# Feed-forward products of a decoder layer: quarters of the tokens (258 columns) in place of thirds (344)

## Chip, cores and metric

The kernel runs on one core of one Trainium2 chip. The metric is the device time of one execution in microseconds (us); the number of a version is the median of several executions. The engines are written PE (TensorE, matrix products), PEld (TensorE's weight loads, which run beside the products), DVE (VectorE), ACT (ScalarE), POOL (GpSimd) and SP (SyncE, which here only issues DMAs).

## The reference, cut to what matters

One inference step of a hybrid decoder layer for a prompt of 1024 tokens and 8 sampled tokens, together T = 1032 tokens, with D_MODEL = 1024 and D_FF = 4096. An input projection, a sparse attention, a state-space branch and a merge come first. The part that the change touches is the feed-forward sub-layer at the end:

```python
def conv_ffn(h, conv_prev, w_up, conv_w, conv_b, w_down):
    up = h @ w_up                                   # (T, 1024) @ (1024, 8192)
    t = up.shape[1]
    ext = jnp.concatenate([conv_prev.astype(up.dtype), up], axis=1)
    acc = conv_b + ext[:, 0:t] * conv_w[0]
    for j in range(1, CONV_W):                      # causal depthwise conv, width 3
        acc = acc + ext[:, j:j + t] * conv_w[j]
    a, b = jnp.split(acc, 2, axis=-1)
    out = (jax.nn.gelu(a) * b) @ w_down             # (T, 4096) @ (4096, 1024)
    return out, ext[:, -(CONV_W - 1):]
```

Its output goes through an RMS norm and is added to the layer's input.

## The kernel before, in words

**Layout.** Activations lie transposed: features on the 128 partitions, the 1032 tokens along the free axis. A product has 128 weights columns as its stationary operand and a run of tokens as its moving operand. Every float32 operand is split in a high part (type fp32r) and the rest (fp32r too), and each product is the sum of three: high by high, high by low, low by high. The split is why every matmul stands three times in the profile, with operands `wh`/`xh`, `wh`/`xl` and `wl`/`xh`.

**project() (line 53; its matmul is recorded as L58).** It makes one unit of output, 128 features by 1032 tokens. The tokens are taken in three chunks of CH = 344 columns; chunk c of the unit in slot s is accumulated in PSUM bank 3s + c. There are two slots, so banks 0 to 5 hold units, and banks 6 and 7 are free for other things. Inside a chunk the loop runs over the kt blocks of 128 input features and the three parts: 3 kt matmuls, each with a weight load of its own in front (PEld). The helper `thirds(ps, slot)` (line 63) views the three banks as one operand for the engine that empties them, and `as_thirds` (line 67) shapes the SBUF side alike.

**phase_ffn (line 2156) and its order.** The 4096 hidden features are taken in NG2 = 16 groups of 256. A group `it` has four "up" units (`ups`, line 2470 on; kt = 8, so 72 matmuls each): a and b halves of two blocks of 128. PE then makes the eight "down" units (`downs`, line 2480 on; kt = 2, so 18 matmuls each) of the group before, which add its 256 hidden features to the 1024 output features. So PE's order is: ups(0), ups(1), downs of group 0, then a hardware loop of 7 turns (`Fori`), two groups a turn, each ups(it) and the downs of it - 1, and at last the downs of group 15. Units alternate between slot 0 and slot 1, and a unit may begin when the one before it in its slot has been emptied.

**Who empties them.** ACT empties an up unit (`evacuate`, L2310) into `up`, and then makes the first of three convolution taps (L2314). DVE makes the other taps (L2380, L2381, L2389), the product of the halves (L2396) and the low part of it (L2401). DVE also empties the down units (`down`, L2410 for the first group, L2412 after): it adds the unit to the running sum `fT`. Where these stand in DVE's queue is written out by hand in `iteration`: down unit 0 goes after the taps of up unit 2; then the middle taps of up unit 3; down unit 1; the last tap of unit 3 and the product; down unit 2; the low part; down units 3 to 7. ACT and POOL make the high and low parts of the streamed weights (L2300, L2254) into two buffers, which SP fills by DMA.

**The end of the phase.** Ten columns of each up unit are kept (POOL, L2261). After the loop PE waits for them, turns eight of the ten by transposes (L2507) into banks 6 and 7, and makes the last eight down units. It then waits until ACT has copied the turned columns (`k_copied`) and turns the other two into bank 7 (L2512). While the last down units come, ACT squares the finished sums, DVE adds the squares up (L2420), PE sums them over partitions into bank 6 (L2516), and at last PE turns `fT` back (L2524), DVE normalises and adds (L2465), and the result is stored. The lines of the end that matter:

```python
            pe.wait_ge(kept_cols, FT)
            for r in range(8):
                mm = pe.transpose(ps[0:FT, 6 + r // 4, (r % 4) * P:(r % 4 + 1) * P], keep[:, r, :], g.ident[:, :])
            mm.then_inc(k_turned, 1)
            downs(NG2, job(NG2, 0), 1, ups_before=False)
            pe.wait_ge(k_copied, 1)
```

Other phases use products of the same type: the input projection with chunks of 344 columns (L1036), the merge (L58 too, with `m_` and `g_y` names), and the output projection (L2112), which has 512 columns a matmul and, for the eight sampled tokens, weights of only 8 columns. L1152 and L1154 are float32 products in the state-space branch, of 128 and of 8 columns.

Of the kernel before, what the change touches and what calls it, by code (L numbers as in the profile page):

```python
# [8 lines left out]
ALU = mybir.AluOpType  # L9
ACT = mybir.ActivationFunctionType  # L10
# [7 lines left out]
KD = D // P  # L18
NP = 1024
NS = 8  # L20
T = NP + NS
# [41 lines left out]
def thirds(ps, slot, m=P):  # L63
    return ps[0:m, 3 * slot:3 * slot + 3, 0:CH]

def as_thirds(ap):
    return ap.rearrange("p (c t) -> p c t", c=3)

def newton_rstd(dve, rstd, std, var, done, base=0):
# [1799 lines left out]
NG2 = FF // P // 2  # L1871
# [284 lines left out]
def phase_ffn(nc, g):  # L2156
# [4 lines left out]
    with ExitStack() as ctx:  # L2161
        sb = lambda n, s, d=F32: ctx.enter_context(nc.sbuf_tensor("f_" + n, s, d))
        ps, sem = g.ps, lambda n: g.sem("f_" + n)
# [119 lines left out]
        def _(act):  # L2283
# [18 lines left out]
            def evacuate(it, q):  # L2302

                u, r = it * 4 + q, q % 2
                tile = bass.ds(it * 2 + (q // 2 + r * (FT // 2)), 1)
                act.wait_ge(up_done, u + 1)
                if not isinstance(it, int) or it or q >= 2:
                    act.wait_ge(conv, u - 1)
                    act.wait_ge(kept_cols, u - 1)
                act.activation(as_thirds(up[:, r, 2:2 + T]), thirds(ps, r), ACT.Copy).then_inc(up_evac, 1)  # L2310
                act.wait_ge(up_evac, u + 1)
                if not isinstance(it, int) or it or q >= 2:
                    act.wait_ge(g_lo, it * 2 + q // 2)
                act.activation(acc[:, r, 0:NP], up[:, r, 0:NP], ACT.Identity, scale=g.cw[:, 0, tile],  # L2314
                               bias=g.cw[:, 3, tile]).then_inc(tap0, 1)
# [58 lines left out]
        @block.vector  # L2374
        def _(dve):
            def tap_mid(it, q):
                u, r = it * 4 + q, q % 2
                tile = bass.ds(it * 2 + (q // 2 + r * (FT // 2)), 1)
                dve.wait_ge(tap0, u + 1)
                dve.tensor_copy(acc[:, r, NP:T], g.conv0[:, tile, :].rearrange("p a b -> p (a b)")).then_inc(tap0s, 1)  # L2380
                dve.scalar_tensor_tensor(out=acc[:, r, 0:NP], in0=up[:, r, 1:1 + NP], scalar=g.cw[:, 1, tile],  # L2381
                                         in1=acc[:, r, 0:NP], op0=ALU.mult, op1=ALU.add).then_inc(tap1, 1)

            def tap_last(it, q):
                u, r = it * 4 + q, q % 2
                tile = bass.ds(it * 2 + (q // 2 + r * (FT // 2)), 1)
                dve.wait_ge(tap0s, u + 1)
                dve.wait_ge(tap1, u + 1)
                dve.scalar_tensor_tensor(out=acc[:, r, :], in0=up[:, r, 2:2 + T], scalar=g.cw[:, 2, tile],  # L2389
                                         in1=acc[:, r, :], op0=ALU.mult, op1=ALU.add).then_inc(conv, 1)  # L2390

            def product(it, r, par):
                m = it * 2 + r
                dve.wait_ge(gelu, m + 1)
                dve.wait_ge(conv, m * 2 + 2)
                dve.tensor_tensor(acc[:, 0, :], acc[:, 0, :], acc[:, 1, :], ALU.mult).then_inc(prod, 1)  # L2396

            def low(it, r, par):
                m = it * 2 + r
                dve.wait_ge(g_hi, m + 1)  # L2400
                dve.tensor_tensor(gl[:, par, r, :], acc[:, 0, :], gh[:, par, r, :].bitcast(F32), ALU.subtract).then_inc(g_lo, 1)  # L2401

            def down(d, m):

                dve.wait_ge(down_done, d + 1)
                if not isinstance(d, int) or d >= 8:
                    dve.wait_ge(down_evac, d - 7)  # L2407
                f = as_thirds(g.fT[:, m, :])
                if isinstance(d, int) and d < 8:
                    dve.tensor_copy(f, thirds(ps, m % 2)).then_inc(down_evac, 1)  # L2410
                else:
                    dve.tensor_tensor(f, thirds(ps, m % 2), f, ALU.add).then_inc(down_evac, 1)  # L2412

            def add_squares(m):

                dve.wait_ge(sq_done, m + 1)
                if m >= 2:
                    dve.wait_ge(sum_done, m - 1)
                other = squares[:, 0, :] if m == 1 else total
                dve.tensor_tensor(total, squares[:, m % 2, :], other, ALU.add).then_inc(sum_done, 1)  # L2420

            def iteration(it, par, has_down):
                for q in range(3):
                    tap_mid(it, q)
                    tap_last(it, q)
                    if q == 1:
                        product(it, 0, par)
                        low(it, 0, par)
                if has_down:
                    down(it * 8 - 8, 0)  # L2430
                tap_mid(it, 3)
                if has_down:
                    down(it * 8 - 7, 1)
                tap_last(it, 3)
                product(it, 1, par)
                if has_down:
                    down(it * 8 - 6, 2)
                low(it, 1, par)
                if has_down:
                    for m in range(3, 8):  # L2440
                        down(it * 8 + (m - 8), m)

            dve.wait_ge(zero, 1)
            iteration(0, 0, False)
            iteration(1, 1, True)
            with dve.Fori(0, (NG2 - 2) // 2) as j:
                for e in range(2):
                    iteration(j * 2 + (2 + e), e, True)
            dve.memset(ones[:, :], 1.0)
            dve.memset(var[:, :], 1.0)  # L2450
            for m in range(8):
                down((NG2 - 1) * 8 + m, m)
                if m >= 2:
                    add_squares(m - 1)
            add_squares(KD - 1)

            dve.wait_ge(ss_done, 1)
            dve.tensor_scalar(var[:, 0:NT], ps[:, 6, 0:NT], 1.0 / D, EPS, ALU.mult, ALU.add).then_inc(ss_copied, 1)
            dve.tensor_scalar(var[0:NS, NT:9], ps[0:NS, 6, NT:9], 1.0 / D, EPS, ALU.mult, ALU.add).then_inc(ss_copied, 1)
            dve.wait_ge(std_done, 1)  # L2460
            newton_rstd(dve, rstd[:, :], std[:, :], var[:, :], r_done, 0)
            for i, (_, n) in enumerate(TILES):
                dve.wait_ge(turned, i + 1)
                dve.wait_ge(x2_in[i % NX], 16 * (i // NX + 1))
                dve.scalar_tensor_tensor(out=x2[0:n, i % NX, :], in0=tile_cols(i), scalar=rstd[0:n, i:i + 1],  # L2465
                                         in1=x2[0:n, i % NX, :], op0=ALU.mult, op1=ALU.add).then_inc(y_done, 1)

        @block.tensor
        def _(pe):
            def ups(it, q, j, s):  # L2470
                u, r = it * 4 + q, q % 2
                pe.wait_ge(w_lo, j + 1)
                if not isinstance(it, int) or it or q >= 2:
                    pe.wait_ge(up_evac, u - 1)
                if q < 2 and (not isinstance(it, int) or it >= 2):
                    pe.wait_ge(down_evac, it * 8 + (q - 9))
                w3, l3 = (w[:, s, :].rearrange("p (k n) -> p k n", k=KD) for w in (wh, wl))
                project(pe, ps, r, w3, l3, g.xT_h, g.xT_l, KD).then_inc(up_done, 1)

            def downs(it, j0, par, ups_before=True):  # L2480

                pe.wait_ge(g_lo, it * 2)
                for m in range(8):
                    if m % 4 == 0:
                        pe.wait_ge(w_lo, j0 + (m // 4 + 1))
                    if m >= 2 or not ups_before:
                        pe.wait_ge(down_evac, it * 8 + (m - 9))
                    else:
                        pe.wait_ge(up_evac, it * 4 + (3 + m))  # L2490
                    w3, l3 = (w[:, m // 4, :].rearrange("p (k n) -> p k n", k=2)[:, :, (m % 4) * P:(m % 4 + 1) * P]
                              for w in (wh, wl))
                    project(pe, ps, m % 2, w3, l3, gh[:, par, :, :], gl[:, par, :, :], 2).then_inc(down_done, 1)

            for q in range(4):
                ups(0, q, q, q % 2)
# [3 lines left out]
            with pe.Fori(0, (NG2 - 2) // 2) as j:  # L2500
                for e in range(2):
                    for q in range(4):
                        ups(j * 2 + (2 + e), q, j * 12 + job(2 + e, q), q % 2)
                    downs(j * 2 + (2 + e), j * 12 + job(2 + e, 4), (1 + e) % 2)
            pe.wait_ge(kept_cols, FT)
            for r in range(8):
                mm = pe.transpose(ps[0:FT, 6 + r // 4, (r % 4) * P:(r % 4 + 1) * P], keep[:, r, :], g.ident[:, :])  # L2507
            mm.then_inc(k_turned, 1)
            downs(NG2, job(NG2, 0), 1, ups_before=False)
            pe.wait_ge(k_copied, 1)  # L2510
            for r in range(8, 10):
                mm = pe.transpose(ps[0:FT, 7, (r - 8) * P:(r - 7) * P], keep[:, r, :], g.ident[:, :])  # L2512
            mm.then_inc(k_turned, 1)
# [192 lines left out]
```

## Time and profile before

| | |
|---|---|
| median of 3 executions | 2284.23 us (2283.46 to 2285.53) |
| the profiled execution's own time | 2281.73 us |
| its span, first to last instruction | 2280.0 us |
| mean granted clock of TensorE over the span | 0.962 of full |
| PE busy | 2089.9 us, 92% |
| PEld busy | 1927.8 us, 85% |
| DVE busy | 1237.3 us, 54% |
| ACT busy | 716.9 us, 31% |
| POOL busy | 528.5 us, 23% |
| feed-forward products, first to last | 1138.4 to 2250.8 us of the span |

The profile gives, for groups of instructions, the busy time, the mean duration of one, and the idle time of the engine ahead of them with what ended it. Durations of matmuls and weight loads hold their latency, and they overlap: two matmuls of 0.32 us each are in flight at any time where one starts every 0.16 us. What a matmul costs in a stream is therefore the distance from one start to the next, not its duration.
### The profile page before, as it was taken

How to read it: one execution, taken by the hardware profiler on the slowest of the kernel's cores; microseconds unless marked ns; L12 is line 12 of the kernel's file. 1: busy time of each engine (PE TensorE's matmuls, PEld its weight loads, DVE VectorE, ACT ScalarE, POOL GpSimd, SP SyncE). 2: the span in 40 equal slices, each digit the busy share in tenths (PEclk: the TensorE clock that was granted, in tenths of full speed). 3: DMA queues.
4: the chain of work that ended last, by engine and by line, in shares of the span. 5: the costliest groups of instructions: out<-in, count | busy, mean ns of one | idle time of the engine just before them, and what ended most of it. 6: DMA issues, size and time to landing. Idle time of an engine off the chain costs nothing. (4 is left out here: it accounts for less than half of the span.)

```text
span 2280.0 us, 33235 instructions
## 1 busy us (share of the span) xinstructions
PE 2089.9 (92%) x13059; PEld 1927.8 (85%) x13059; DVE 1237.3 (54%) x2033; ACT 716.9 (31%) x1065; POOL 528.5 (23%) x417
## 2 busy tenths in 40 slices
PE   3999999999668987979699999999999999999997
PEld 2968888899555644977499999999999999999997
DVE  4657999899247630425535444444344454344455
ACT  3234333322236631124333322223222233222233
POOL 0223334222015320230012222222222222222220
PEclk7999999999779978989899999999999999999998
DMA  3311232223320032433111111111111111111123
GB/s 110 76 38 55 83 90 71 81 76 93 108 82 6 2 135 79 140 126 114 39 46 56 47 47 42 43 56 41 43 47 47 47 47 47 47 47 41 53 84 109
DMA packets 177155, 150.62 MB, mean 66 GB/s; under 512 B 29458, under 2 KB 150834, under 8 KB 176994
## 3 DMA queue, kind: packets, MB, share of 16 engines
q1 hardware_dynamic: 175722, 144.21, 20.8%
q0 software_dynamic: 1280, 4.20, 0.5%
q8 instruction: 117, 1.92, 0.4%
q14 instruction: 36, 0.29, 0.0%
HBM read 119.53 MB, written 27.93 MB: 65 GB/s over the span
## 5 line engine op out<-in xcount | busy, mean ns | idle before, releaser
L58 PE MATMUL ps<-g_xT_h,f_wh 128*128 128x344 f32 x1536 | 492.8, 321 | 7.3 <-issue 6.4
L58 PE MATMUL ps<-g_xT_l,f_wh 128*128 128x344 f32 x1536 | 491.3, 320 | 0.0
L58 PE MATMUL ps<-g_xT_h,f_wl 128*128 128x344 f32 x1536 | 491.2, 320 | 0.0
L2254 POOL TENSOR_TENSOR f_wl<-f_wst,f_wh 128x1024 fp32r<-128x1024 f32 x94 | 244.8, 2605 | 383.1 <-ACT f_wh L2300 383.1
L58 PEld LDWEIGHTS ps<-g_xT_h,f_wh 128*128 128x128 f32 x1536 | 289.1, 188 | 9.1 <-issue 9.0
L58 PEld LDWEIGHTS ps<-g_xT_h,f_wl 128*128 128x128 f32 x1536 | 289.3, 188 | 0.0
L58 PEld LDWEIGHTS ps<-g_xT_l,f_wh 128*128 128x128 f32 x1536 | 289.0, 188 | 0.0
L1036 PE MATMUL ps<-g_hT_h,j_wh 128*128 128x344 f32 (+1 forms) x840 | 285.3, 340 | 0.2 <-POOL j_wl L636 0.2
L1036 PE MATMUL ps<-g_hT_h,j_wl 128*128 128x344 f32 (+1 forms) x840 | 269.6, 321 | 0.0
L1036 PE MATMUL ps<-g_hT_l,j_wh 128*128 128x344 f32 (+1 forms) x840 | 269.6, 321 | 0.0
L58 PE MATMUL ps<-f_gh,f_wh 128*128 128x344 f32 x768 | 248.8, 324 | 7.5 <-DVE g_fT L2412 6.9
L2412 DVE TENSOR_TENSOR g_fT<-ps,g_fT 128x1032 f32<-128x1032 f32 x120 | 147.6, 1230 | 185.3 <-PE ps L58 185.3
L58 PE MATMUL ps<-f_gl,f_wh 128*128 128x344 f32 x768 | 246.0, 320 | 0.0
L58 PE MATMUL ps<-f_gh,f_wl 128*128 128x344 f32 x768 | 245.4, 319 | 0.0
L2380 DVE COPY f_acc<-g_conv 128x8 f32 (+1 forms) x64 | 35.6, 557 | 363.5 <-ACT f_acc L2314 363.5
L2310 ACT ACTIVATE f_up<-ps 128x1032 f32<-128x1032 f32 x64 | 66.2, 1034 | 448.3 <-PE ps L58 448.3
L636 POOL TENSOR_TENSOR j_wl<-j_wst,j_wh 128x1024 fp32r<-128x1024 f32 (+1 forms) x35 | 85.0, 2427 | 404.5 <-ACT j_wh L710 404.5
L2389 DVE SCALAR_TENSOR_TENSOR f_acc<-f_up,g_cw,f_acc 128x1032 f32<-128x1032 f32 x64 | 170.4, 2662 | 10.7 <-DVE f_acc L2381 10.0
L1036 PEld LDWEIGHTS ps<-g_hT_h,j_wh 128*128 128x128 f32 (+1 forms) x840 | 157.9, 188 | 19.4 <-issue 17.3
L889 DVE TENSOR_SCALAR_CACHE_REDUCE j_rel<-g_masks,j_cand 128x384 uint8<-128x384 f32 (+2 forms) x192 | 169.0, 943 | 1.1
L1036 PEld LDWEIGHTS ps<-g_hT_l,j_wh 128*128 128x128 f32 (+1 forms) x840 | 158.1, 188 | 4.3 <-issue 3.8
L1036 PEld LDWEIGHTS ps<-g_hT_h,j_wl 128*128 128x128 f32 (+1 forms) x840 | 157.8, 188 | 0.5
(408 smaller groups left out, 3340.7 us busy)
## 6 DMA issues: line engine op xcount, KB each, us to landing
f_wst<-in_w_up SPq DMA_DIRECT2D x64, 512.0 KB, 4.1
j_wst<-in_w_in SPq DMA_DIRECT2D x34, 512.0 KB, 4.3
f_wst<-in_w_down SPq DMA_DIRECT2D x32, 512.0 KB, 3.7
d_gates<-j_ring SPq DMA_DIRECT2D x16, 516.0 KB, 3.0
m_gt<-d_gates SPq DMA_DIRECT2D x16, 516.0 KB, 4.8
n_x<-in_x_prompt SPq DMA_DIRECT2D x8, 512.0 KB, 7.7
a_v<-in_cache_v POOLq DMA_DIRECT2D x16, 256.0 KB, 7.3
a_k<-in_cache_k SPq DMA_DIRECT2D x16, 256.0 KB, 3.1
```

The lines of the kernel that those rows point to most:

```text
L58: mm = pe.matmul(ps[0:m, 3 * slot + c, 0:CH], w[:, k, 0:m], x[:, k, c * CH:(c + 1) * CH], start=(first and k == 0 and n == 0), stop=(last ...
L636: pool.tensor_tensor(wl[:, s, :, 0:n], wst[:, s, :, 0:n], wh[:, s, :, 0:n].bitcast(F32), ALU.subtract).then_inc(w_lo, 1)
L889: dve.tensor_scalar(hit(q), keys(q), limits(q), None, op, ALU.add, accum_out=count[:, q:q + 1]).then_inc(counted, 1)
L1036: mm = pe.matmul(ps[0:n, t % 2, 0:CH], w[:, s, k, 0:n], x[:, k, c * CH:(c + 1) * CH], start=(k == 0 and q == 0), stop=(k == KD - 1 and q = ...
L2254: pool.tensor_tensor(wl[:, s, :], wst[:, s, :], wh[:, s, :].bitcast(F32), ALU.subtract).then_inc(w_lo, 1)
L2310: act.activation(as_thirds(up[:, r, 2:2 + T]), thirds(ps, r), ACT.Copy).then_inc(up_evac, 1)
L2380: dve.tensor_copy(acc[:, r, NP:T], g.conv0[:, tile, :].rearrange("p a b -> p (a b)")).then_inc(tap0s, 1)
L2389: dve.scalar_tensor_tensor(out=acc[:, r, :], in0=up[:, r, 2:2 + T], scalar=g.cw[:, 2, tile], in1=acc[:, r, :], op0=ALU.mult, op1=ALU.add). ...
L2412: dve.tensor_tensor(f, thirds(ps, m % 2), f, ALU.add).then_inc(down_evac, 1)
```

## The change

A new helper `project4` makes the same unit in four chunks of T // 4 = 258 columns, with chunk c of the unit in slot s in bank 4s + c: two slots now take all eight banks. `quarters` and `as_quarters` are the views of four banks for the engines that empty them. The up and down units of the feed-forward phase use them; the merge and the other phases keep `project`. A unit has 96 matmuls in place of 72 (up) and 24 in place of 18 (down). Since banks 6 and 7 now belong to slot 1, three waits are added or changed at the end of the phase: the first eight transposes wait until all down units of the loop have been emptied; the second of the last down units waits for ACT's copy of the turned columns; the last two transposes wait until the last down unit has been emptied, in place of the wait for that copy.

```diff
--- before.py
+++ after.py
@@ -66,6 +66,25 @@
 
 def as_thirds(ap):
     return ap.rearrange("p (c t) -> p c t", c=3)
+
+
+def project4(pe, ps, slot, wh, wl, xh, xl, kt):
+
+    n = T // 4
+    for c in range(4):
+        for k in range(kt):
+            for q, (w, x) in enumerate(((wh, xh), (wh, xl), (wl, xh))):
+                mm = pe.matmul(ps[:, 4 * slot + c, 0:n], w[:, k, :], x[:, k, c * n:(c + 1) * n],
+                               start=(k == 0 and q == 0), stop=(k == kt - 1 and q == 2))
+    return mm
+
+
+def quarters(ps, slot):
+    return ps[:, 4 * slot:4 * slot + 4, 0:T // 4]
+
+
+def as_quarters(ap):
+    return ap.rearrange("p (c t) -> p c t", c=4)
 
 
 def newton_rstd(dve, rstd, std, var, done, base=0):
@@ -2307,7 +2326,7 @@
                 if not isinstance(it, int) or it or q >= 2:
                     act.wait_ge(conv, u - 1)
                     act.wait_ge(kept_cols, u - 1)
-                act.activation(as_thirds(up[:, r, 2:2 + T]), thirds(ps, r), ACT.Copy).then_inc(up_evac, 1)
+                act.activation(as_quarters(up[:, r, 2:2 + T]), quarters(ps, r), ACT.Copy).then_inc(up_evac, 1)
                 act.wait_ge(up_evac, u + 1)
                 if not isinstance(it, int) or it or q >= 2:
                     act.wait_ge(g_lo, it * 2 + q // 2)
@@ -2405,11 +2424,11 @@
                 dve.wait_ge(down_done, d + 1)
                 if not isinstance(d, int) or d >= 8:
                     dve.wait_ge(down_evac, d - 7)
-                f = as_thirds(g.fT[:, m, :])
+                f = as_quarters(g.fT[:, m, :])
                 if isinstance(d, int) and d < 8:
-                    dve.tensor_copy(f, thirds(ps, m % 2)).then_inc(down_evac, 1)
+                    dve.tensor_copy(f, quarters(ps, m % 2)).then_inc(down_evac, 1)
                 else:
-                    dve.tensor_tensor(f, thirds(ps, m % 2), f, ALU.add).then_inc(down_evac, 1)
+                    dve.tensor_tensor(f, quarters(ps, m % 2), f, ALU.add).then_inc(down_evac, 1)
 
             def add_squares(m):
 
@@ -2475,7 +2494,7 @@
                 if q < 2 and (not isinstance(it, int) or it >= 2):
                     pe.wait_ge(down_evac, it * 8 + (q - 9))
                 w3, l3 = (w[:, s, :].rearrange("p (k n) -> p k n", k=KD) for w in (wh, wl))
-                project(pe, ps, r, w3, l3, g.xT_h, g.xT_l, KD).then_inc(up_done, 1)
+                project4(pe, ps, r, w3, l3, g.xT_h, g.xT_l, KD).then_inc(up_done, 1)
 
             def downs(it, j0, par, ups_before=True):
 
@@ -2486,11 +2505,13 @@
                         pe.wait_ge(w_lo, j0 + (m // 4 + 1))
                     if m >= 2 or not ups_before:
                         pe.wait_ge(down_evac, it * 8 + (m - 9))
+                        if m == 1:
+                            pe.wait_ge(k_copied, 1)
                     else:
                         pe.wait_ge(up_evac, it * 4 + (3 + m))
                     w3, l3 = (w[:, m // 4, :].rearrange("p (k n) -> p k n", k=2)[:, :, (m % 4) * P:(m % 4 + 1) * P]
                               for w in (wh, wl))
-                    project(pe, ps, m % 2, w3, l3, gh[:, par, :, :], gl[:, par, :, :], 2).then_inc(down_done, 1)
+                    project4(pe, ps, m % 2, w3, l3, gh[:, par, :, :], gl[:, par, :, :], 2).then_inc(down_done, 1)
 
             for q in range(4):
                 ups(0, q, q, q % 2)
@@ -2503,11 +2524,12 @@
                         ups(j * 2 + (2 + e), q, j * 12 + job(2 + e, q), q % 2)
                     downs(j * 2 + (2 + e), j * 12 + job(2 + e, 4), (1 + e) % 2)
             pe.wait_ge(kept_cols, FT)
+            pe.wait_ge(down_evac, (NG2 - 1) * 8)
             for r in range(8):
                 mm = pe.transpose(ps[0:FT, 6 + r // 4, (r % 4) * P:(r % 4 + 1) * P], keep[:, r, :], g.ident[:, :])
             mm.then_inc(k_turned, 1)
             downs(NG2, job(NG2, 0), 1, ups_before=False)
-            pe.wait_ge(k_copied, 1)
+            pe.wait_ge(down_evac, NG2 * 8)
             for r in range(8, 10):
                 mm = pe.transpose(ps[0:FT, 7, (r - 8) * P:(r - 7) * P], keep[:, r, :], g.ident[:, :])
             mm.then_inc(k_turned, 1)
```

## Rows read from the trace of the kernel before

**Rows 1.** The profile's first page: the span, and busy time by engine.

```profile
span 2280.0 us, 33235 instructions
...
PE 2089.9 (92%) x13059; PEld 1927.8 (85%) x13059; DVE 1237.3 (54%) x2033; ACT 716.9 (31%) x1065; POOL 528.5 (23%) x417
```

**Rows 2.** Busy time of each engine in the feed-forward stretch; then clock, DMA share, GB/s.

```profile
1138.40:2250.80 1112.40, 1098.34 (x6922) 1090.72 (x6922) 519.19 (x391) 318.06 (x302) 257.77 (x159) 1.00 0.16 48
```

**Rows 3.** Waits of PE, 1200 to 2230 us: total us, times, longest.

```profile
PE ps L58 <- DVE g_fT L2412: 6.9, 14, 0.5
PE ps L58 <- issue: 6.4, 6, 1.2
```

**Rows 4.** Timeline around 1308 us, one group's stall: start, us, engine, line.

```profile
1304.01 1.83 DVE L2380 COPY f_acc<-g_conv 128x8 f32 x1
...
1309.41 1.23 DVE L2396 TENSOR_TENSOR f_acc<-f_acc 128x1032 f32<-128x1032 f32 x1
1310.57 1.23 DVE L2412 TENSOR_TENSOR g_fT<-ps,g_fT 128x1032 f32<-128x1032 f32 x1
...
1311.84 0.42 PE L58 MATMUL ps<-f_gh,f_wh 128*128 128x344 f32 x1 [0.50 <-DVE g_fT L2412]
```

**Rows 5.** Groups by line: one of three parts of the up products, and its loads.

```profile
L58 PE MATMUL ps<-g_xT_h,f_wh 128*128 128x344 f32 x1536 | 492.8, 321 | 7.3 <-issue 6.4
...
L58 PEld LDWEIGHTS ps<-g_xT_h,f_wh 128*128 128x128 f32 x1536 | 289.1, 188 | 9.1 <-issue 9.0
```

**Rows 6.** Stretches, PE alone: length, busy (instructions), granted clock, DMA share, GB/s.

```profile
1139.00:1141.60 2.60, 2.60 (x11) 0.50 0.60 170
1016.00:1029.00 13.00, 13.00 (x58) 1.00 0.49 166
1314.00:1374.00 60.00, 60.00 (x383) 1.00 0.15 45
```

**Rows 7.** Timeline, 512 columns, weights of 128 columns; 27 such rows left out.

```profile
1016.34 0.63 PE L2112 MATMUL ps<-o_wl,g_xT_h 128*128 128x512 f32 x2
...
1029.38 0.63 PE L2112 MATMUL ps<-o_wh,g_xT_l 128*128 128x512 f32 x2
```

**Rows 8.** Timeline, 512 columns, weights of 8 columns; 20 such rows left out.

```profile
1109.28 0.61 PE L2112 MATMUL ps<-o_wl,g_xT_h 128*8 128x512 f32 x2
...
1118.98 0.62 PE L2112 MATMUL ps<-o_wl,g_xT_h 128*8 128x512 f32 x2
```

**Rows 9.** Timeline, first feed-forward products, 344 columns at half clock; 6 rows left out.

```profile
1139.16 0.49 PE L58 MATMUL ps<-g_xT_h,f_wl 128*128 128x344 f32 x1
...
1141.17 0.49 PE L58 MATMUL ps<-g_xT_h,f_wh 128*128 128x344 f32 x1
```

**Rows 10.** Timeline, products of 128 and of 8 columns with full weights.

```profile
427.99 1.05 PE L1152 MATMUL ps<-j_u,g_kT 128*128 128x128 f32 x8
428.88 0.96 PE L1154 MATMUL ps<-j_u,g_kT 128*128 128x8 f32 x8
429.69 0.40 PE L1036 MATMUL ps<-g_hT_h,j_wh 128*128 128x344 f32 x1
```

**Rows 11.** Timeline, weight loads after a stall, with the array empty.

```profile
1311.84 0.19 PEld L58 LDWEIGHTS ps<-f_gh,f_wh 128*128 128x128 f32 x1 [0.78 <-DVE g_fT L2412]
...
1311.95 0.19 PEld L58 LDWEIGHTS ps<-f_gl,f_wh 128*128 128x128 f32 x1
```

**Rows 12.** Groups by line: the two evacuations of PSUM.

```profile
L2412 DVE TENSOR_TENSOR g_fT<-ps,g_fT 128x1032 f32<-128x1032 f32 x120 | 147.6, 1230 | 185.3 <-PE ps L58 185.3
...
L2310 ACT ACTIVATE f_up<-ps 128x1032 f32<-128x1032 f32 x64 | 66.2, 1034 | 448.3 <-PE ps L58 448.3
```

**Rows 13.** Timeline of the end: transposes, last evacuation of the loop, sum of squares.

```profile
2226.63 0.92 PEld L2507 LDWEIGHTS ps<-g_ident,f_keep 128*64 128x64 f32 x8
...
2227.07 1.23 DVE L2412 TENSOR_TENSOR g_fT<-ps,g_fT 128x1032 f32<-128x1032 f32 x1 [1.60 <-PE ps L58]
...
2254.34 3.35 PE L2516 MATMUL ps<-f_ones,f_acc 128*128 128x1 f32 x18 [3.59 <-DVE f_acc L2420]
```

## The prediction, made blind

> **What bounds the kernel now.** I read the first page before anything else: PE is busy for 92% of the span and no other engine for more than 54% [rows 1]. An average says little about one phase, so next the table of stretches over the feed-forward products alone: 1112.40 us, PE busy for 1098.34 of them at full granted clock, DVE for 519, ACT for 318 [rows 2]. The reader is to see that nothing but PE's own stream can matter there. Then PE's waits: in 1030 us of that phase it waits 6.9 us for DVE, in 14 pieces of at most 0.5 us, and 6.4 us at six loop ends for nothing that the profile shows [rows 3]. So the phase is a count of matmuls times the distance between their starts, and that distance is what I need for 258 columns. No chunk of that size and type is in the trace.
>
> **The distance between starts.** The duration of 321 ns [rows 5] is not it. In 60.00 us without a gap 383 matmuls touch the stretch, two of them in flight at its edges: 60.00 / 381 = 157.5 ns for 344 columns, at clock 1.00 [rows 6]. With 512 columns 56 starts take 1029.38 - 1016.34 = 13.04 us: 232.9 ns, at clock 1.00 too [rows 6, 7]. The line through both has a slope of (232.9 - 157.5) / 168 = 0.449 ns a column and 3.1 ns that each matmul pays whatever its size. At 258 columns it gives 3.1 + 115.8 = **118.9 ns**. One block of features and one of the three parts (a "pair") cost 3 x 157.5 = 472.5 ns before and will cost 4 x 118.9 = 475.6 ns: **+3.1 ns a pair**.
>
> The bounds of that. Below: all is paid by the column. At the rate of 344 columns, 0.458 ns, a matmul takes 118.1 ns and a pair changes by 0; at the rate of 512 columns, 0.455 ns, 117.4 ns and -2.9 ns a pair. Above: at half clock 344 columns start 2.01 / 7 = 287 ns apart [rows 9], which is 344 columns at 1.2 GHz and nothing more; at 2.4 GHz they would need 143.3 ns and take 14.2 more. If all these 14.2 ns were paid by the matmul, 258 columns would take 107.5 + 14.2 = 121.7 ns, +14.3 ns a pair. I take the line, since 512 columns pay 232.9 - 213.3 = 19.6 ns over: the surplus grows nearly with the columns.
>
> The Trainium skill has a rule that speaks against small matmuls here (TensorE: Matmul & The Clock Gate, "Back-to-back issue gap"): columns at 2.4 GHz and about 2.5 ns for each matmul. By it a pair goes from 3 x 145.8 to 4 x 110.0 ns, +2.5 ns, and my sum below would end at 2291.0. The trace does not agree on the level, 157.5 ns where the rule has 145.8, but its part paid by the matmul is of the size of my 3.1 ns.
>
> **Weight loads.** Each matmul has its own load, so these go from 6912 to 9216. Products of 128 columns start (428.88 - 427.99) / 8 = 111 ns apart and those of only 8 columns 101 ns [rows 10]: there the load of 128 weight columns sets the distance. After a stall two loads start 0.11 us apart [rows 11]. A load every 111 ns fits under a matmul every 118.9 ns, with 8 ns to spare. And 512 columns behind loads of 8 columns are 9.70 / 42 = 231.0 ns apart [rows 8], 1.9 ns less than behind full ones: loads cost the stream at most that, and it is part of the 3.1 ns.
>
> **How many pairs count.** Up units: 64 with 24 pairs, 1536; down units: 128 with 6, 768. In 15 of the 16 rounds of down units (14 of them in rows 3, the first is like them) PE stalls before down unit 4, because DVE comes late to down unit 2 [rows 4]: DVE's chain starts when down unit 0 is done and runs on its own clock (POOL's work holds its short copy for 1.83 us, then taps, product and down unit 2), while PE makes units 1 to 3. What these three units gain in length, up to the 0.5 us of the stall, the stall loses. That takes 15 x 3 x 6 = 270 pairs out: 2304 - 270 = 2034 pairs x 3.1 ns = **+6.3 us**.
>
> **Evacuations.** They read four runs of 258 in place of three of 344. DVE takes 1.230 us for three runs out of PSUM [rows 12] and 1.23 us for one run in SBUF [rows 4], so a run costs nothing that shows: 0. ACT's evacuation waits 448.3 us for PE in all [rows 12]; were it 0.1 us longer, this wait would cover it. On DVE 0.1 us in each of down units 0 to 2 would lengthen the stall by up to 0.3 us x 15 = 4.5 us; I keep that for the range.
>
> **The loop ends.** The loop body has a third more instructions. If the 6.4 us of rows 3 grew with it: +2.1 us. The trace ties it to nothing, so 0, and 2.1 for the range.
>
> **The three waits at the end.** The first eight transposes were loaded at 2226.63, while DVE still had the last down unit of the loop to empty, until 2227.07 + 1.23 = 2228.30 [rows 13]. Now they wait for that. PE follows a DVE release by 0.04 us (1310.57 + 1.23, then 1311.84 [rows 4]), so 2228.34: **+1.7 us**, and all behind it moves along: only the last eight down units and the end. POOL, SP and DVE hold nothing that this wait delays first. The second wait is for ACT's copy of the turned columns, about 1 us as its other PSUM copies [rows 12]; the first of the last down units covers it with 24 x 118.9 ns = 2.85 us. Without that cover it would cost 1 us once. The third is over when the last down unit is emptied, and PE has to wait for DVE's squares after that anyway, until 2254.34 [rows 13]: 0. These products run partly after an idle PE; whether the clock of the last stretch changes is open, some 1.4 us either way (18 small matmuls took 3.35 us, 186 ns each, where a load needs 111 at most [rows 10, 13]: 18 x 75 ns).
>
> **Sum.** 6.3 + 1.7 = +8.0 us on the profiled execution, whose own time is 2281.73 us around a span of 2280.0 [rows 1]; it lies 2.5 us under the median of the runs. On the median: 2284.23 + 8.0 = **2292.2 us**. About 0.2%, 4.6 us, is what a measurement of this kernel can tell from no change: "same" is 2279.7 to 2288.8.
>
> **The rivals.**
> - *Columns alone are paid; not slower.* If 258 columns take 118.1 ns, the products cost the same and only the new wait at the end is left: 2285.9; at 117.4 ns it is 2280.0. For it: the surplus over 2.4 GHz is 14.2 / 344 = 0.041 ns a column at 344 and 19.6 / 512 = 0.038 at 512, near enough to constant. Against it: the rest of 1.9 ns between loads of 8 and of 128 columns, which comes once a matmul. It decides from 118.5 ns down, since 4.6 - 1.7 = 2.9 us over 2034 pairs are 1.4 ns a pair. My 118.9 lies close above that.
> - *The surplus is paid by the matmul.* 121.7 ns; 2034 x 14.3 = 29.1, with the wait 30.8: 2315.0. Against it are 512 columns, which pay 19.6 and not 14.2 ns [rows 7]; for it, that 512 and 344 are both longer than anything that the change uses, and the line is drawn out beyond them.
> - *Loads show.* If the 1.9 ns double because a load now fills 111 of 119 ns: 4 x 1.9 = 7.6 ns a pair, +15.5 us on top: 2307.7. In its full form the loads set the distance and it stays at 157.5 ns: 2034 x 157.5 = +320 us, 2606. Against the full form are rows 8 and 10. The Trainium skill (Perfetto Trace Analysis, "Identifying the Most-Contended Engine") says that the busy share of LDWEIGHTS tells how near PE is to its limit; here it is 1090.72 of 1112.40 us [rows 2], and a third more loads could not fit. The trace does not agree: a load lasts 188 ns [rows 5] and starts 111 ns after another.
> - *The surplus shrinks in short chunks; faster.* At half of it by the column, 107.5 + 5.3 = 112.8 ns, just above the loads' 111: 21.3 ns less a pair, 2034 x 21.3 = -43 us, 2242.6. For it: the loads allow it. Against it: from 512 to 344 columns the surplus a column rises.
>
> **How the numbers follow.** Forecast 0.42 (2288.8 to 2300); columns alone 0.33; by the matmul 0.12; loads 0.06; faster 0.07. Faster 0.07, same 0.33, slower 0.42 + 0.12 + 0.06 = 0.60. The forecast and the first rival have most of the chance, so the range runs from 2281, just over that rival's lower end, to 2316, which holds the costs paid by the matmul, the loop ends and a longer evacuation. Left out are the faster case, the full form of the loads, and thin ends: under 2 in 10.
>
> **What would show it.** A gap-free stretch of 60 us should hold 60.00 / 0.1189 + 2 = 507 matmuls of 258 columns at clock 1.00; 495 would be the price by the matmul, 510 columns alone. The feed-forward stretch should be 1112.4 + 8 = 1120.4 us. L2412 should stay at 1.23 us and L2310 at 1.03; PE's wait for L2412 in the loop should shrink a little; one new wait of 1.7 us should stand before the first transposes. I am wrong if the distance is off 118 to 119.5 ns, or if PE waits for DVE for more than 0.7 us a group.

## The result, and the profile after

The median went from 2283.85 to **2305.82 us**: ratio 1.009, 95% interval 1.0072 to 1.0108. The medians differ by +22.0 us, and the interval stands for +16 to +25, where +8.0 were forecast. The direction and the range (2281 to 2316) hold; the size is off by a factor of about 2.7, and this section says where it came from. The profiled execution took 2305.15 us.

The first page of the changed kernel, against [rows 1]; the group of [rows 5], with the idle time of PE ahead of it after the bar; and the stretch of the feed-forward products and a gap-free 60 us of it (columns as in [rows 2]):

```profile
span 2303.5 us, 37845 instructions
...
PE 2112.1 (92%) x15363; PEld 1951.4 (85%) x15363; DVE 1237.0 (54%) x2033; ACT 717.2 (31%) x1065; POOL 528.1 (23%) x417
...
L77 PE MATMUL ps<-g_xT_h,f_wh 128*128 128x258 f32 x2048 | 581.6, 284 | 11.7 <-DVE g_fT L2431 10.9
```

```profile
1138.40:2274.70 1136.30, 1116.73 (x9224) 1112.13 (x9224) 518.73 (x392) 318.28 (x302) 257.57 (x159) 0.99 0.16 47
1315.00:1375.00 60.00, 60.00 (x503) 60.00 (x502) 22.65 (x17) 15.64 (x16) 14.07 (x9) 1.00 0.15 45
```

All of the time is in that stretch: 1112.4 us before, 1136.3 now. No other engine works longer. In 60 us there are 503 matmuls; one lasts 284 ns, so 2.4 are in flight at the edges, and the starts are 60.00 / 500.6 = 119.9 ns apart. Taken from the starts themselves, over 9106 distances without a stall, the mean is **119.8 ns** (before, over 6842: 157.5).

Next the turn of PE's loop, which I had costed at nothing. The first line is the branch at the loop's end as the trace has it for PE's sequencer, seven times with its shortest, median and longest duration in ns; then the timeline of the first turn and its table of stretches (length, busy, granted clock, DMA share, GB/s):

```profile
L2521 PEldq COMPARE_BRANCH  x7: 76/3618/3812, 1393.6 to 2246.6; - x7
```

```profile
1395.48 0.28 PE L77 MATMUL ps<-f_gh,f_wl 128*128 128x258 f32 x1
...
1395.88 1.23 DVE L2431 TENSOR_TENSOR g_fT<-ps,g_fT 128x1032 f32<-128x1032 f32 x1 [1.62 <-PE ps L77]
...
1397.58 0.38 PE L77 MATMUL ps<-g_xT_h,f_wh 128*128 128x258 f32 x1 [1.82 <-DVE g_fT L2431]
```

```profile
1315.00:1375.00 60.00, 60.00 (x503) 1.00 0.15 45
1395.80:1397.50 1.70, 0.00 (x0) 1.00 0.00 0
1398.40:1401.80 3.40, 3.40 (x18) 0.50 0.25 66
1402.00:1412.00 10.00, 10.00 (x86) 1.00 0.08 25
```

And the same in the kernel before, whose rows had this branch too:

```profile
L2500 PEldq COMPARE_BRANCH  x7: 76/3533/3742, 1389.5 to 2224.2; - x7
```

```profile
1392.07 0.32 PE L58 MATMUL ps<-f_gh,f_wl 128*128 128x344 f32 x1
...
1393.43 0.42 PE L58 MATMUL ps<-g_xT_h,f_wh 128*128 128x344 f32 x1 [1.04 <-issue]
```

The reader is to see three things. The branch back takes 3.5 to 3.6 us in both kernels, and the sequencer reaches it ahead of the array: in the first turn it starts at 1393.6, while the last matmul ahead of it starts at 1395.48, 1.9 us later, or 16 x 119.8 ns. Before these were 1389.5 and 1392.07, 2.6 us, or 16 x 157.5 ns. So 16 queued matmuls cover part of the branch, and shorter matmuls cover less of it. In all twelve turns of the two kernels the next matmul starts 0.38 to 0.43 us after the branch has ended. Second, the profile names DVE's L2431 for this wait, but the code waits there only for the last down unit but one (`it * 8 + (q - 9)` with q = 0), whose evacuation was long over; DVE's end at 1397.11 just lies nearest. Third, the clock falls to 0.50 after some of these waits: 18 matmuls touch the 3.4 us, where full clock fits about 30. In this execution that happened behind three of the six turns.

At the end of the phase, against [rows 13], the new wait stands where it was foreseen:

```profile
2248.90 1.23 DVE L2431 TENSOR_TENSOR g_fT<-ps,g_fT 128x1032 f32<-128x1032 f32 x1 [1.66 <-PE ps L77]
...
2250.25 0.80 PEld L2529 LDWEIGHTS ps<-g_ident,f_keep 128*64 128x64 f32 x8 [1.69 <-issue]
```

Where the +23.4 us between the first and the last of these products come from (1111.8 to 1135.2 us), summed over the starts in the two traces:

| | before | after | difference, us |
|---|---|---|---|
| distance of matmuls, 2304 pairs | 472.5 ns | 479.1 ns | +15.3 |
| six turns, idle beyond one distance | 7.4 us | 11.8 us | +4.4 |
| half clock behind turns | none | three times | +4.5 |
| wait between loop and last down units | 0.8 us | 2.5 us | +1.7 |
| stalls before down units 3 and 4, with the loads behind them | 12.7 us | 10.3 us | -2.4 |

### The profile page after: what moved, and what is told of

Its sections match the earlier page's. It is cut to its first block and busy times, and to the rows that moved or that the text cites. A ratio compares the mean times of both kernels' runs of the same rounds, so it can differ in the third digit from the quotient of the medians.

```text
span 2303.5 us, 37845 instructions
## 1 busy us (share of the span) xinstructions
PE 2112.1 (92%) x15363; PEld 1951.4 (85%) x15363; DVE 1237.0 (54%) x2033; ACT 717.2 (31%) x1065; POOL 528.1 (23%) x417
## 5 line engine op out<-in xcount | busy, mean ns | idle before, releaser
L77 PE MATMUL ps<-g_xT_h,f_wh 128*128 128x258 f32 x2048 | 581.6, 284 | 11.7 <-DVE g_fT L2431 10.9
L77 PE MATMUL ps<-g_xT_h,f_wl 128*128 128x258 f32 x2048 | 581.5, 284 | 0.0
L77 PE MATMUL ps<-g_xT_l,f_wh 128*128 128x258 f32 x2048 | 579.9, 283 | 0.0
L77 PEld LDWEIGHTS ps<-g_xT_h,f_wh 128*128 128x128 f32 x2048 | 389.8, 190 | 13.0 <-DVE g_fT L2431 12.1
L77 PE MATMUL ps<-f_gh,f_wh 128*128 128x258 f32 x1024 | 291.0, 284 | 6.3 <-DVE g_fT L2431 5.9
L77 PE MATMUL ps<-f_gh,f_wl 128*128 128x258 f32 x1024 | 289.1, 282 | 0.0
L77 PE MATMUL ps<-f_gl,f_wh 128*128 128x258 f32 x1024 | 288.9, 282 | 0.0
L2431 DVE TENSOR_TENSOR g_fT<-ps,g_fT 128x1032 f32<-128x1032 f32 x120 | 147.6, 1230 | 192.2 <-PE ps L77 192.2
L77 PEld LDWEIGHTS ps<-f_gh,f_wh 128*128 128x128 f32 x1024 | 192.9, 188 | 9.4 <-DVE g_fT L2431 8.7
L77 PEld LDWEIGHTS ps<-f_gl,f_wh 128*128 128x128 f32 x1024 | 193.8, 189 | 0.0
L77 PEld LDWEIGHTS ps<-f_gh,f_wl 128*128 128x128 f32 x1024 | 193.5, 189 | 0.0
```

The costliest lines, as they stand in the source:

```text
L77: mm = pe.matmul(ps[:, 4 * slot + c, 0:n], w[:, k, :], x[:, k, c * n:(c + 1) * n], start=(k == 0 and q == 0), stop=(k == kt - 1 and q == 2))
L2431: dve.tensor_tensor(f, quarters(ps, m % 2), f, ALU.add).then_inc(down_evac, 1)
```

## The experiments

Ten kernels ran. Three questions were open: why 258 columns take 119.8 and not 118.9 ns; whether a turn costs what its rows suggest; and what stalls would be left. The edits are to the changed kernel where it is called quarters, to the kernel before where it is called thirds.

**Why 119.8 ns: four runs, one execution of each.**

narrow_loads, and the same edit on thirds as thirds_narrow:

```diff
+                m = P if q == 0 or (k == kt - 1 and q == 2) else P // 2
-                mm = pe.matmul(ps[:, 4 * slot + c, 0:n], w[:, k, :], ...
+                mm = pe.matmul(ps[0:m, 4 * slot + c, 0:n], w[:, k, 0:m], ...
```

> Quarters, but two of the three parts of each product (high by low and low by high, except the one that closes a chunk) use only the first 64 of the 128 weight columns: their loads are half as long, the matmuls stream the same 258 columns. It leaves out the small corrections for half of the features. Theory loads: a matmul of 258 columns is held by the load in front of it, so with short loads in two of three places the distance falls from 119.8 ns to 118.9 or less. Theory matmul: the extra is paid by each matmul whatever its load, so it stays at 119.8 within 0.3. Theory addresses: it stays at 119.8 too.

> Thirds, with the short loads of narrow_loads (64 of 128 weight columns in two of the three parts, except the one that closes a chunk; the small corrections for half of the features are left out). It tells whether a load costs the stream the same beside any matmul. Theory corner: a load costs more the nearer its 111 ns come to the matmul's own length, so at 344 columns the distance behind short loads falls by only 0.5 to 0.9 ns (157.5 to 156.6 to 157.0), less than the 1.3 ns at 258 columns. Rival, even cost: it falls by 1.3 ns here too, to 156.2, and loads don't explain what 258 columns take over the line.

even_starts:

```diff
-                mm = pe.matmul(..., x[:, k, c * n:(c + 1) * n],
+                mm = pe.matmul(..., x[:, k, c * 256:c * 256 + n],
```

> Quarters of 258 columns that start every 256 columns (1024 bytes) in place of every 258 (1032 bytes), so that each chunk starts where the chunks of 344 could start too, at a multiple of 32 bytes; six columns are computed twice and the last six tokens are left out. Theory addresses: the distance between starts falls from 119.8 ns to 118.9 or less, some 2304 x 4 x 0.9 ns = 8 us less in all. Theories loads and matmul: 119.8 within 0.3, and the same time as quarters.

four_widths:

```diff
+                o, n = ((0, 160), (160, 232), (392, 296), (688, 344))[c]
-                mm = pe.matmul(..., x[:, k, c * n:(c + 1) * n],
+                mm = pe.matmul(..., x[:, k, o:o + n],
```

> Quarters with chunks of 160, 232, 296 and 344 columns in place of four of 258 (the sum is the same 1032; the evacuation still takes 258 columns of each bank, so that the output holds other values). By the line of the prediction: 111 ns for 160 columns (the load's own pace), 111 for 232 (the load again; the line gives 107.3), 136.0 for 296, 157.5 for 344. Theory loads: 232 columns take more than 111, 113 to 116 ns, because load and matmul get into each other's way when they are nearly as long, and 296 columns take 136.0. Theory matmul: a cost of about 1 ns more than the line's at every width under 344, so 296 columns take 136.5 to 137 ns and 232 columns 111.

Gap-free stretches of 60 us of narrow_loads, even_starts and thirds_narrow, in this order (PE alone: busy, instructions, clock, DMA share, GB/s):

```profile
1316.00:1376.00 60.00, 60.00 (x506) 1.00 0.16 45
```

```profile
1317.00:1377.00 60.00, 60.00 (x503) 1.00 0.15 45
```

```profile
1316.00:1376.00 60.00, 60.00 (x384) 1.00 0.15 45
```

Then four_widths, the first matmul of each chunk of 24, from the last chunk of one up unit (344 columns) through the next unit; of 160 and 232 columns the second matmul too:

```profile
1352.17 0.32 PE L78 MATMUL ps<-g_xT_h,f_wh 128*128 128x344 f32 x1
...
1355.94 0.24 PE L78 MATMUL ps<-g_xT_h,f_wh 128*128 128x160 f32 x1
1356.02 0.28 PE L78 MATMUL ps<-g_xT_l,f_wh 128*128 128x160 f32 x1
...
1358.59 0.31 PE L78 MATMUL ps<-g_xT_h,f_wh 128*128 128x232 f32 x1
1358.73 0.27 PE L78 MATMUL ps<-g_xT_l,f_wh 128*128 128x232 f32 x1
...
1361.31 0.30 PE L78 MATMUL ps<-g_xT_h,f_wh 128*128 128x296 f32 x1
...
1364.56 0.32 PE L78 MATMUL ps<-g_xT_h,f_wh 128*128 128x344 f32 x1
```

*Addresses* falls: with even starts 503 matmuls are in 60 us as before, and the mean distance is 120.0 ns. (Its time, 2313.76 us, is longer than that of quarters mostly because the clock fell behind all six turns.)

In four_widths the chunks shown take 157.1, 110.4, 113.3 and 135.4 ns a matmul. The line of the prediction is good at 296 columns (135.9; 136.1 measured over the whole phase) and 0.9 ns short at 258. At 160 and 232 columns the load is the bound. That 232 look slower than 160 comes from one matmul of each chunk: the second matmul starts 0.08 us after the first at 160 columns and 0.14 us after it at 232. The 23 behind it are 111.7 and 112.2 ns apart here, and over all up units 111.7 and 111.9. So 232 columns do not take the 113 to 116 ns of theory loads, and 296 do not take the 136.5 to 137 of theory matmul. Neither explains what 258 columns take.

The short loads don't settle it either. In narrow_loads, two matmuls in a row with short loads start 118.5 ns apart, 1.3 less than the mean in quarters; in thirds_narrow 157.0, 0.5 less than the mean in thirds. That is the difference that theory corner expected. But against the same two parts of the product in quarters and in thirds the falls are 0.9 and 0.6 ns, and the mean over all matmuls, short and full loads together, falls alike: by 0.6 ns to 119.2 in the one and by 0.55 ns to 156.95 in the other. The edit also halves the features that these matmuls write, and no run separates that from the loads. So the two together are worth some tenths of a nanosecond beside any matmul; that they explain the 0.9 ns is not shown. It stays open.

**The wait at the end alone: thirds_waits**, thirds with the three changed waits.

```diff
             pe.wait_ge(kept_cols, FT)
+            pe.wait_ge(down_evac, (NG2 - 1) * 8)
...
+                        if m == 1:
+                            pe.wait_ge(k_copied, 1)
...
-            pe.wait_ge(k_copied, 1)
+            pe.wait_ge(down_evac, NG2 * 8)
```

> Thirds, with the three changed waits of the end alone. Theory: the first eight transposes wait 1.7 us for the last evacuation of the loop and all behind moves along: +1.7 us, ratio 1.0007. Rival: the end has slack, or TensorE's clock in the last stretch goes the other way: 0 us. Rival: the idle 1.7 us drops the granted clock to half for some microseconds of the last down units: +3 us or more.

Ratio 1.0013, interval 1.0003 to 1.0023: +0.7 to +5.3 us, which holds the 1.7 and leaves out 0. The trace is sharper. Columns as in [rows 13]; first the kernel before, then thirds_waits:

```profile
2226.63 0.32 PE L58 MATMUL ps<-f_gh,f_wl 128*128 128x344 f32 x1
...
2227.57 0.41 PE L58 MATMUL ps<-f_gh,f_wh 128*128 128x344 f32 x1
```

```profile
2225.08 0.32 PE L58 MATMUL ps<-f_gh,f_wl 128*128 128x344 f32 x1
...
2225.53 1.23 DVE L2412 TENSOR_TENSOR g_fT<-ps,g_fT 128x1032 f32<-128x1032 f32 x1 [1.60 <-PE ps L58]
...
2226.91 1.03 PE L2510 MATMUL ps<-g_ident,f_keep 128*64 128x128 f32 x8 [1.51 <-DVE g_fT L2412]
...
2227.70 0.40 PE L58 MATMUL ps<-f_gh,f_wh 128*128 128x344 f32 x1
```

From the start of the loop's last matmul to the start of the first of the last down units pass 2.62 us, against 0.95 before: 1.67 us. The clock stayed full in between.

**The turns: quarters_flat, thirds_flat, quarters_body4.** The first two have the same edit, the third another body:

```diff
-            with pe.Fori(0, (NG2 - 2) // 2) as j:
+            for j in range((NG2 - 2) // 2):
                 for e in range(2):
```

```diff
-            with pe.Fori(0, (NG2 - 2) // 2) as j:
-                for e in range(2):
+            for e in range(2):
+                for q in range(4):
+                    ups(2 + e, q, job(2 + e, q), q % 2)
+                downs(2 + e, job(2 + e, 4), (1 + e) % 2)
+            with pe.Fori(0, (NG2 - 4) // 4) as j:
+                for e in range(4):
                     for q in range(4):
-                        ups(j * 2 + (2 + e), q, j * 12 + job(2 + e, q), q % 2)
-                    downs(j * 2 + (2 + e), j * 12 + job(2 + e, 4), (1 + e) % 2)
+                        ups(j * 4 + (4 + e), q, j * 24 + job(4 + e, q), q % 2)
+                    downs(j * 4 + (4 + e), j * 24 + job(4 + e, 4), (1 + e) % 2)
```

> Quarters, with PE's loop of seven turns written out, so that PE takes no branch back. Theory turn: each of the six turns costs about 2.0 us of idle PE (the branch takes 3.6 us, and the 16 matmuls queued ahead of it last 16 x 119.8 ns = 1.9), and about 1.6 us more where the clock falls to half behind it; without the branch all of this goes: 6 x 1.97 + 3.7 = 15.5 us less, 2290. Rival, fetching: straight code has to be fetched too and stalls as often: no change, 2306. Rival, DVE: the wait that the profile names at the turn (DVE's evacuation) is real and stays: no change, 2306.

> Thirds with the same loop written out. Theory turn: six waits of 1.24 us less, and 0.6 us at the first matmuls: 8 us less, 2276. With quarters_flat the difference of the two should be the spacing alone, 2304 x (4 x 119.8 - 3 x 157.5) = 15.4 us, and the wait at the end, 1.7, less the shorter stalls, 2.4: 14 to 15 us. Rivals as for quarters_flat: 2284.

> Quarters, with two groups ahead of the loop and a body of four groups in place of two: three turns, two branches back, the body twice as long. Theory turn: what a turn costs does not depend on the length of the body: two waits of about 2.0 us, and the time falls by 4 x 1.97 us and by 4/6 of the 3.7 us at half clock: 10.3 us less, 2295.5. Rival, length: the wait grew from 1.24 to 1.97 us because the body grew by a third, so with twice the body it is 4.2 us: two waits of 4.2 us, 3.4 us less, 2302.

| | median, us | ratio to before, interval | expected, us |
|---|---|---|---|
| quarters_flat | 2290.73 | 1.0028 (1.0016 to 1.0039) | 2290 |
| thirds_flat | 2276.29 | 0.9964 (0.9954 to 0.9974) | 2276 |
| quarters_body4 | 2294.09 | 1.0047 (1.003 to 1.0064) | 2295.5 |

PE's waits for DVE, quarters_flat first, then quarters_body4:

```profile
PE ps L77 <- DVE g_fT L2431: 7.1, 14, 0.6
```

```profile
PE ps L77 <- DVE g_fT L2431: 10.1, 16, 2.1
```

Without the branch the waits of 2 us are gone, so they were not DVE's, and so is the half clock inside the phase. Straight code does not stall. With a body twice as long two waits are left, of 2.2 us each beyond one distance and not of 4.2: a turn does not cost by the length of its body. Turns with what hangs on them cost quarters 2305.82 - 2290.73 = 15.1 us and thirds 2283.48 - 2276.29 = 7.2 us. What is left between the two written-out kernels, 14.4 us, is the distance, the wait at the end and the stalls: 15.3 + 1.7 - 2.4 = 14.6.

**A version that beats both: thirds_flat_order and thirds_flat_order2.** With the turns gone, the stall of [rows 4] was the largest idle time left.

```diff
                 tap_last(it, 3)
+                if has_down:
+                    down(it * 8 - 6, 2)
                 product(it, 1, par)
-                if has_down:
-                    down(it * 8 - 6, 2)
                 low(it, 1, par)
```

> Thirds with the loop written out, and in DVE's queue the emptying of down unit 2 put ahead of the product of the halves. Theory: the stall of 0.66 us before down unit 4, 15 times, comes from DVE's queue order (the product's 1.23 us stand ahead of the emptying that PE waits for), so it goes: 15 x 0.77 us (with the first load after it) = 11 us less than thirds_flat, 2265. Rival: the next wait takes its place (down unit 1, emptied just in time before down unit 3, or the product late for the next units): 3 us less or none.

It gave 2283.71 us, 7 us more than thirds_flat: the rival, and worse than it said. DVE's queue in one group:

```profile
1450.69 1.22 DVE L2412 TENSOR_TENSOR g_fT<-ps,g_fT 128x1032 f32<-128x1032 f32 x1
1451.84 1.22 DVE L2396 TENSOR_TENSOR f_acc<-f_acc 128x1032 f32<-128x1032 f32 x1
1454.19 1.23 DVE L2401 TENSOR_TENSOR f_gl<-f_acc,f_gh 128x1032 fp32r<-128x1032 f32 x1 [1.13 <-ACT f_gh L2327]
1455.34 1.22 DVE L2412 TENSOR_TENSOR g_fT<-ps,g_fT 128x1032 f32<-128x1032 f32 x1
```

Unit 2 comes in time, but the low part (L2401) now waits 1.13 us for ACT's high part, with down unit 3 queued behind it, and PE stalls for that instead, before down unit 5. The old order had filled this gap with unit 2. So unit 3 goes into it:

```diff
                 tap_last(it, 3)
+                if has_down:
+                    down(it * 8 - 6, 2)
                 product(it, 1, par)
                 if has_down:
-                    down(it * 8 - 6, 2)
+                    down(it * 8 - 5, 3)
                 low(it, 1, par)
                 if has_down:
-                    for m in range(3, 8):
+                    for m in range(4, 8):
                         down(it * 8 + (m - 8), m)
```

> Thirds with the loop written out, and in DVE's queue down unit 2 ahead of the product and down unit 3 between the product and its low part. Theory: in thirds_flat_order the stall went from down unit 4 to down unit 5, because DVE waited for ACT's high part with down unit 3 queued behind it; with unit 3 in that gap no stall is left, and 15 x 0.86 us = 13 us go: 2263. Rival: the low part or a later unit is late next, or the idle DVE was needed elsewhere: within 3 us of thirds_flat, 2276.

It gave **2264.95 us**, where 2263 was expected; ratio 0.9918 (0.9901 to 0.9936): 11.3 us under thirds_flat and 40.9 under the changed kernel. PE has no wait left in the phase that the profile would list. The new order was run on thirds alone; what it is worth with quarters isn't known.

## Why the prediction was right, and where it fell short

- *What bounds it.* Right: the time is PE's stream; DVE, ACT and POOL did not change, L2431 takes 1230 ns as [rows 12] and the evacuation of four runs cost nothing.
- *The distance.* The first failed step: 118.9 ns was forecast and 119.8 measured, outside the 118 to 119.5 ns that the prediction itself named as the sign of being wrong. A pair costs +6.6 ns and not +3.1: +15.3 us over 2304 pairs, or +12.9 with what the stalls gave back, in place of +6.3. The mechanism, a small part paid by each matmul on top of the columns, held at 296 columns; at 258 the term was mis-sized by 0.9 ns, and no run shows why. The rivals at either end fell: by the column alone would be 118.1 ns, by the matmul 121.7. "Loads show" would be 120.8 in its small form; half of that was measured, and no run shows that it is the loads.
- *Loads.* Right that they fit: at 160 columns matmuls with full loads start 111.7 ns apart in this stream too. The Trainium skill judges how near PE is to its limit by the matmul work done and by the busy share of LDWEIGHTS (Perfetto Trace Analysis, "Identifying the Most-Contended Engine"). The trace does not agree on the second: by it this phase had no room for a third more loads, and it took them for 2% more time, as PEld's 1090.72 of 1112.40 us [rows 2] became 1112.13 of 1136.30.
- *The loop ends.* "The trace ties it to nothing, so 0": wrong, and it is the second failed step and the larger one. It is tied to the branch, which has rows of its own that I had not read. With the clock it is +8.9 us here, of the 15.4 that the forecast was short in this execution, and the bound that I kept, 2.1, did not hold it. The written-out kernels show it: the turns are worth 15.1 us in quarters and 7.2 in thirds.
- *The clock.* The prediction looked for a change of clock at the end of the phase and not within it. It fell behind the idle 2 us of a turn in three of six turns here; before, behind 1.2 us, in none. What decides in which turns it falls is not shown.
- *The wait at the end.* +1.7 us forecast, 1.67 measured.
- *The stall that gives some back.* Right in kind: taken out as 270 pairs, which is 0.8 us at the forecast 3.1 ns, and measured as 2.4 us.
- *Chances.* 0.60 on slower was sound: by my numbers the main term was only 1.7 ns a pair from "same". That the time lies in the range is partly luck. The two errors went the same way, away from "same", and the range reached to 2316 mostly for other costs, a surplus paid by the matmul and a longer evacuation, which did not come.

## What to carry to other kernels

Ask for the spacing of matmuls start to start, from a stretch without gaps, and treat a line through two widths with care beyond them: here it was right at 296 columns and 0.9 ns short at 258, some 8 us over 9216 matmuls. Look at the sequencer's rows of a hardware loop: a branch of 3.5 us is hidden only by the work that is queued ahead of it, so smaller matmuls make the same loop dearer, and writing the loop out paid 7 to 15 us here. An engine's queue order that looks arbitrary can fill another's gap; move one unit, and look at what stands behind the next wait.

## What was not expected of the hardware

- A branch back on PE takes 3.3 to 3.8 us in both kernels, 3.5 and 3.6 on the median. 16 matmuls were queued ahead of it, of 344 or of 258 columns, and cover 2.6 or 1.9 us.
- The granted clock fell from 1.00 to 0.50 for some 16 matmuls behind turns with about 2 us of idle PE: in 3 of 6 turns of quarters, 6 of 6 of even_starts, 2 of 6 of narrow_loads and 1 of 2 of quarters_body4. The length of the wait alone does not decide it, since the turn of quarters_body4 that kept its clock idled 2.2 us, no less than the other. It never fell behind the 1.7 us of thirds_waits, the 1.4 to 1.7 us of four_widths or the 1.2 us of thirds.
- The distance at full clock for fp32r products with full loads: 111.7 ns (160 columns) and 111.9 (232), each behind the first matmul of its chunk in up units, 119.8 (258), 136.1 (296), 157.5 (344), 232.9 (512).
